# The norm tails of a two-layer hybrid block: the root taken on ScalarE straight from PSUM, token factors spread by repeated-column matmuls, residual adds dealt to GpSimd and VectorE in turn

## The reference

```python
def rmsnorm(x, g):
    y = xf * lax.rsqrt(jnp.mean(xf * xf, axis=-1, keepdims=True) + EPS)
    return y * g
def modulate(h, g_pre, shift, scale):
    return rmsnorm(h, g_pre) * (1 + scale) + shift
def gated_residual(h, y, g_post, gate, weight):
    return h + weight * gate * rmsnorm(y, g_post)
def swiglu_half(h, m, k, g_pre, g_post, wg, wu, wd):
    u = modulate(h, g_pre, m[3 * k], m[3 * k + 1])
    y = (jax.nn.silu(u @ wg) * (u @ wu)) @ wd
    return gated_residual(h, y, g_post, m[3 * k + 2], MACARON_WEIGHT)
# each layer: swiglu_half, then a mixer (state-space scan, two gated convolutions, output product)
# with its own modulate and gated_residual, then swiglu_half again; m comes from silu(c) @ w_mod + b_mod
```

## Time and profile before

| What | Value |
|---|---|
| Median of 3 runs | 2484.2 us (2481.6 to 2488.03) |
| The profiled execution: own time | 2481.05 us |
| The profiled execution: span of the rows | 2479.3 us |
| Instructions in it | 28910 |
| TensorE busy | 2263.5 us, 91% |
| VectorE busy | 1303.8 us, 53% |
| ScalarE busy | 986.9 us, 40% |
| GpSimd busy | 74.9 us, 3% |

### The profile page before, as it was taken

How to read it: one execution, slowest core, us unless ns; L and a number is a source line. 1 busy time by engine, 2 the same in 40 slices (tenths; PEclk the granted TensorE clock), 3 DMA queues, 4 the chain that set the end, 5 groups by cost and what they waited for, 6 DMA issues and landing times. The chain is left out here.

```text
span 2479.3 us, 28910 instructions
## 1 busy us (share of the span) xinstructions
PE 2263.5 (91%) x11863; PEld 1909.0 (77%) x11863; DVE 1303.8 (53%) x1785; ACT 986.9 (40%) x1479; POOL 74.9 (3%) x80
## 2 busy tenths in 40 slices
PE   5899999978998989799999997999996988978998
PEld 5788888757686767578888875888885866877997
DVE  4544444267958834544444435333325587855554
ACT  4544334244342343444433444223324442355443
POOL 0000000010101000100000001000001001000000
PEclk8999999978999989799999997999997899988999
DMA  6445544211211112244554441323321221233653
GB/s 211 145 161 170 161 158 150 93 53 51 68 35 41 49 65 85 68 153 158 165 169 155 160 144 51 102 91 96 128 94 53 69 85 52 79 109 119 188 183 124
DMA packets 275347, 278.36 MB, mean 112 GB/s; under 512 B 7487, under 2 KB 274447, under 8 KB 275215
## 3 DMA queue, kind: packets, MB, share of 16 engines
q1 hardware_dynamic: 274419, 274.32, 34.8%
q10 hardware_dynamic: 795, 2.18, 0.2%
HBM read 275.44 MB, written 1.05 MB: 112 GB/s over the span
## 5 line engine op out<-in xcount | busy, mean ns | idle before, releaser
L95 DVE TENSOR_TENSOR split<-raw,split 128x1024 fp32r<-128x1024 f32 (+1 forms) x368 | 442.7, 1203 | 744.7 <-ACT split L87 744.6
L87 ACT ACTIVATE split<-raw 128x1024 fp32r<-128x1024 f32 (+1 forms) x368 | 383.0, 1041 | 909.4 <-PE bank L128 897.4
L126 PE MATMUL bank<-uh,split 128*128 128x512 f32 (+1 forms) x1344 | 490.2, 365 | 1.2 <-DVE split L95 1.2
L128 PE MATMUL bank<-uh,split 128*128 128x512 f32 (+1 forms) x1344 | 489.3, 364 | 0.0
L127 PE MATMUL bank<-ul,split 128*128 128x512 f32 (+1 forms) x1344 | 487.5, 363 | 0.0
L128 PEld LDWEIGHTS bank<-uh,split 128*128 128x128 f32 x1344 | 252.4, 188 | 42.3
L126 PEld LDWEIGHTS bank<-uh,split 128*128 128x128 f32 x1344 | 252.5, 188 | 38.6 <-issue 1.5
L127 PEld LDWEIGHTS bank<-ul,split 128*128 128x128 f32 x1344 | 252.2, 188 | 38.8
L126 PE MATMUL bank<-mix_uh,split 128*128 128x512 f32 (+1 forms) x608 | 234.0, 385 | 32.3 <-DVE split L95 17.2
L126 PE MATMUL bank<-hh,split 128*128 128x512 f32 (+1 forms) x704 | 257.4, 366 | 1.0 <-DVE split L95 1.0
L127 PE MATMUL bank<-hl,split 128*128 128x512 f32 (+1 forms) x704 | 256.0, 364 | 0.0
(11 more groups left out here) (227 smaller groups left out, 2807.5 us busy)
## 6 DMA issues: line engine op xcount, KB each, us to landing
raw_mod<-in_w_mod SPq DMA_DIRECT2D x64, 1024.0 KB, 5.0
raw<-in_ffn_w_gate SPq DMA_DIRECT2D x44, 1024.0 KB, 5.3
raw<-in_ffn_w_up SPq DMA_DIRECT2D x44, 1024.0 KB, 5.3
raw<-in_w_in SPq DMA_DIRECT2D x40, 1024.0 KB, 5.3
raw<-in_ffn_w_down SPq DMA_DIRECT2D x32, 1024.0 KB, 5.2
raw<-in_w_out SPq DMA_DIRECT2D x16, 1024.0 KB, 5.2
raw<-in_ffn_w_down SPq DMA_DIRECT2D x16, 768.0 KB, 4.4
stage<-in_w_mod SPq DMA_DIRECT2D x6, 1024.0 KB, 12.3
```

The lines of the kernel that those rows point to most:

```text
L87: ins = K.nc.scalar.activation(K.wh[:, half, 0:kn, :], K.raw[:, slot, 0:kn, half * P:half * P + P], ACT.Copy)
L95: ins = K.nc.vector.tensor_tensor(K.wl[:, half, 0:kn, :], K.raw[:, slot, 0:kn, half * P:half * P + P], r32(K.wh[:, half, 0:kn, :]), ALU.su ...
L126: K.nc.tensor.matmul(bank[:, 0:tn], K.wh[:, half, k, :], h, start=first and k == 0, stop=False)
L128: ins = K.nc.tensor.matmul(bank[:, 0:tn], K.wl[:, half, k, :], h, start=False, stop=last and k == kn - 1)
```

## The change

There are four edits.

1. The norm factor. ScalarE now takes the root of sum/width + EPS directly from `bank[5]` (EPS as a bias tile that GpSimd fills in the opening), VectorE the reciprocal of the result into `rstd`.
2. The spread. No diagonal is built. Four matmuls (two with 256 tokens) take column t of `rstd`, repeated 128 times, as weights and the 128x128 identity as moving tile, and write 128 columns of `bank[6]` each.
3. The residual. VectorE multiplies all 8 tiles as before, but tiles 2, 5 and 7 go to `bank[0]` to `bank[2]`, and VectorE adds each from there to `K.res` right away. GpSimd adds tiles 0, 1, 3, 4 and 6.
4. The `gain` for the next phase's norm is formed in the `OutProduct` before (in the opening for the first), not at the head of the phase.

```diff
-def rstd_dve(K, dve, tok, width, stats, nth):
+def rstd_act(K, act, tok, width, stats, nth):
     n = tok[1] // P
-    dve.wait_ge(K.stat_done.sem, K.stat_done.at(stats))
-    ins = K.nc.vector.tensor_scalar(K.ms[:, 0:n], K.bank[5][:, 0:n], 1.0 / width, EPS, ALU.mult, ALU.add)
-    ins.then_inc(K.dve_step.inc(), 1)
-    dve.wait_ge(K.dve_step.sem, K.dve_step.own())
-    K.nc.vector.reciprocal(K.ms[:, 0:n], K.ms[:, 0:n]).then_inc(K.ms_ready.inc(), 1)
-    dve.wait_ge(K.rstd_ready.sem, K.rstd_ready.at(nth))
-    ins = K.nc.vector.tensor_tensor(
-        K.diag[:, 0:n, :], K.ident[:, :].unsqueeze(1).to_broadcast([P, n, P]),
-        K.rstd[:, 0:n].unsqueeze(2).to_broadcast([P, n, P]), ALU.mult)
-    ins.then_inc(K.diag_ready.inc(), 1)
-
-
-def rstd_act(K, act, tok, nth):
+    act.wait_ge(K.stat_done.sem, K.stat_done.at(stats))
+    ins = K.nc.scalar.activation(K.ms[:, 0:n], K.bank[5][:, 0:n], ACT.Sqrt, scale=1.0 / width, bias=K.eps[:, 0:1])
+    ins.then_inc(K.ms_ready.inc(), 1)
+
+
+def rstd_dve(K, dve, tok, nth):
     n = tok[1] // P
-    act.wait_ge(K.ms_ready.sem, K.ms_ready.at(nth))
-    K.nc.scalar.activation(K.rstd[:, 0:n], K.ms[:, 0:n], ACT.Sqrt).then_inc(K.rstd_ready.inc(), 1)
+    dve.wait_ge(K.ms_ready.sem, K.ms_ready.at(nth))
+    if nth > 1:
+        dve.wait_ge(K.rb_ready.sem, K.rb_ready.at(nth - 1))
+    K.nc.vector.reciprocal(K.rstd[:, 0:n], K.ms[:, 0:n]).then_inc(K.rstd_ready.inc(), 1)
 
 
 def rstd_pe(K, pe, tok, nth):
 
-    n = tok[1]
-    pe.wait_ge(K.diag_ready.sem, K.diag_ready.at(nth))
-    ins = K.nc.tensor.matmul(K.bank[6][:, 0:n], K.ones[:, :],
-                             K.diag[:, 0:n // P, :].rearrange("p t n -> p (t n)"), start=True, stop=True)
+    pe.wait_ge(K.rstd_ready.sem, K.rstd_ready.at(nth))
+    for t in range(tok[1] // P):
+        ins = K.nc.tensor.matmul(K.bank[6][:, t * P:t * P + P], K.rstd[:, t:t + 1].to_broadcast([P, P]), K.ident[:, :],
+                                 start=True, stop=True)
     ins.then_inc(K.rb_ready.inc(), 1)
...
+def pre_gain_dve(K, dve, layer, which):
+
+    nc = K.nc
+    scale = K.mod[:, layer, 8 * (3 * which + 1):8 * (3 * which + 2), :]
+    dve.wait_ge(K.mod_evac.sem, K.mod_evac.own())
+    nc.vector.tensor_scalar(K.gain[:, :, :], scale, 1.0, None, ALU.add).then_inc(K.dve_step.inc(), 1)
+    dve.wait_ge(K.dve_step.sem, K.dve_step.own())
+    g = K.par[:, layer, 0, 72 + 8 * which:80 + 8 * which].unsqueeze(2).to_broadcast([P, 8, 2])
+    nc.vector.tensor_tensor(K.gain[:, :, :], K.gain[:, :, :], g, ALU.mult).then_inc(K.dve_step.inc(), 1)
...
-POOL_TILES = 5
+POOL_TILES = (0, 1, 3, 4, 6)
+OWN_TILES = (2, 5, 7)
...
-    normed(range(6))
-    pair(0)
-    normed((6, 7))
-    add(range(POOL_TILES, 6))
-    pair(1)
-    add((6, 7))
-    pair(2)
-    pair(3)
+    own = 0
+    for j in range(8):
+        if j in POOL_TILES:
+            K.nc.vector.tensor_tensor(y[:, j, 0:tn], y[:, j, 0:tn], K.bank[6][:, 0:tn], ALU.mult).then_inc(K.yr_ready.inc(), 1)
+            continue
+        part = K.bank[own][:, 0:tn]
+        own += 1
+        K.nc.vector.tensor_tensor(part, y[:, j, 0:tn], K.bank[6][:, 0:tn], ALU.mult).then_inc(K.yb_ready.inc(), 1)
+        dve.wait_ge(K.yb_ready.sem, K.yb_ready.at(own))
+        ins = K.nc.vector.tensor_tensor(K.res[:, j, t0:t0 + tn], K.res[:, j, t0:t0 + tn], part, ALU.add)
+        ins.then_inc(K.res_tail.inc(), 1)
+        if j == 5:
+            pair(0)
+    for i in range(1, 4):
+        pair(i)
...
+            if n == 2 and self.next_norm:
+                pre_gain_dve(K, dve, *self.next_norm)
```

More of the change, by code:

```diff
@@ L329, in normed @@
         ins.then_inc(K.un_ready.inc(), 1)
[L332 to L337, removed]
     normed(0)
@@ L378, in post_tile_dve, with residual_dve @@
     K.nc.vector.tensor_tensor(total, total, more, ALU.add).then_inc(K.sq_added.inc(), 1)
-POOL_TILES = 5
-def residual_dve(K, dve, tok, y, stats, nth, norm_follows, norms_before):
+POOL_TILES = (0, 1, 3, 4, 6)
+OWN_TILES = (2, 5, 7)
+def residual_dve(K, dve, tok, y, nth, norm_follows, norms_before):
     t0, tn = tok
[L388 to L396, removed]
     def pair(i):
@@ L447, with __init__ @@
 class OutProduct:
-    def __init__(self, K, w, parts, order, xh, xl, tok, xtok, y, halves, panels, stats, norms, norm_follows, gain, mods=0,
+    def __init__(self, K, w, parts, order, xh, xl, tok, xtok, y, halves, panels, stats, norms, next_norm, gain, mods=0,
                  mod_h=0, mod_layer=0, mod_q=0):
@@ L459, in __init__ @@
         self.mods, self.mod_h, self.mod_layer, self.mod_q = mods, mod_h, mod_layer, mod_q
-        self.norm_follows, self.gain = norm_follows, gain
+        self.next_norm, self.norm_follows, self.gain = next_norm, bool(next_norm), gain
         self.mod_group = 1 if mod_h else 0
@@ L532, in act @@
                 post_tile_act(K, act, K.bank[2 * (j // 2 % 2) + j % 2], j, self.tok, self.y)
-        rstd_act(K, act, self.tok, self.norms)
+        rstd_act(K, act, self.tok, 1024, self.stats + 1, self.norms)
         if self.norm_follows:
             split_ahead_act(K, act)
-            residual_rms_act(K, act, self.tok, self.y, self.norms + 1)
+            residual_rms_act(K, act, self.tok, self.y, self.stats + 1, self.norms + 1)
     def dve(self, dve, skip=0):
@@ L557, in dve, with feed_forward @@
             mod_out_dve(K, dve, self.mod_layer, self.mod_q, self.mods // 2, self.mod_group)
-        residual_dve(K, dve, self.tok, self.y, self.stats + 1, self.norms, self.norm_follows, self.norms - 1)
+        residual_dve(K, dve, self.tok, self.y, self.norms, self.norm_follows, self.norms - 1)
         if self.norm_follows:
-            residual_rms_dve(K, dve, self.tok, self.stats + 1, self.norms + 1)
-def feed_forward(K, layer, which, tok, mod_layer, mod_q, mods_loop, mods_down, following):
+            split_ahead_dve(K, dve)
+            rstd_dve(K, dve, self.tok, self.norms + 1)
+def feed_forward(K, layer, which, tok, mod_layer, mod_q, mods_loop, mods_down, following, next_norm):
     nc = K.nc
@@ L1149, in _ @@
                         pass
-            rstd_act(K, act, part, 1)
+            rstd_act(K, act, part, GRP_T * P, GRP_T, 1)
             split_ahead_act(K, act)
@@ L1421, in _ @@
                     ins.then_inc(K.xbc_conv.inc(), 1)
-            rstd_dve(K, dve, part, GRP_T * P, GRP_T, 1)
+            rstd_dve(K, dve, part, 1)
             dve.wait_ge(K.rb_ready.sem, K.rb_ready.at(1))
@@ L1627, in _ @@
             nc.gpsimd.memset(K.cond[:, :].bitcast(F32), 0.0).then_inc(K.const_step.inc(), 1)
+            nc.gpsimd.memset(K.eps[:, :], EPS).then_inc(K.const_step.inc(), 1)
             n = K.const_step.count
@@ L1922, in hybrid_block @@
             feed_forward(K, layer, 2, LATENT if last else FULL, None if last else layer + 1, 0, not last,
-                         0 if last else 24, after)
+                         0 if last else 24, after, None if last else (layer + 1, 0))
         closing(K)
```

43 lines of the change are left out of this document (20 added, 23 removed).

## The result

The changed kernel takes **2499.4 us** (median of 5 runs, 2493.6 to 2504.2) against 2484.2 us: ratio 1.0058 (of the means, here and below), interval 1.0037 to 1.0079. It is slower by 0.6% where 0.8% less was predicted. The profiled execution took 2500.53 us, its span 2498.8.

The account below looks back on a forecast made before the run. TensorE, busy 91% of the span, bounds the kernel, so only its idle time can be won: 11.9 + 2.3 + 4.9 − 0.7 + 0.6 = 19.0 us off the 2484.2 us median gives 2465 us, range 2458 to 2477.

Parts of the forecast that it names:

- The signature: Sign that the prediction is wrong: intervals from barrier to barrier shortened while the phases between them grew; no size given.
- Norm gap: From last sum to factor spread in 16 norms: root on ScalarE without a diagonal shortens TensorE's wait, 11.9 us won.
- Spread: Factor spread on TensorE: four 128-column matmuls take less time than one of 512 columns, 2.3 us won.
- `gain`: Heads of phases: forming the pre-norm gain ahead of the barrier takes L333 and L336 off the path, 4.9 us won.
- Residual, tails with a norm: First multiply to pair 1 in four 512-token tails: the new order makes the stage 0.2 us longer each, 0.7 us lost.
- Residual, last tail: End of the kernel, where nothing follows: the new residual order shortens it from 4.75 to 4.1, 0.6 us won.
- more of the spreads fall ahead of the clock's fall: Upper bound for the four-matmul form: 5 us won if the earlier start brings two more spreads ahead of the clock's fall.
- the walk: VectorE's new residual order followed operation by operation from the first multiply: pair 1 done at 8.75 us.
- rival 1: Multiplies into PSUM ahead of pair 1 in the tails are dear: 10.8 us come in full, 2476 us; chance 0.08.
- rival 3: VectorE from first multiply to pair 1: PSUM write and add reading it both slow, about 2488 us at x = 0.75; chance 0.03.
- Rival 2, the clock: TensorE's restarts in tails and pauses meet the clock's course differently: 7 us of gain given back, 2472 us; chance 0.09.

Follow-up runs that it names:

- −64 bytes: Kernel before with only the small tensor gain allocated ahead of split, so the distance from weights to moving tensors is 64 bytes shorter: 2478.6 us, ratio 0.9977.

## Why the prediction was wrong

The step that failed is not a term of the sum. It is that the sum has none for the products: it takes 19 us off the profiled span and lets all else stand. EPS was read as "a bias tile that GpSimd fills in the opening", hence work of an instruction, and its 32 bytes were never counted. They moved every moving operand against the weights. The bodies paid 28.0 us for it (2225.2 against 2197.2 with EPS in `ms`), the dead tile alone 29 by the medians. None of the four rivals had it. The signature stood in the prediction, "the intervals from barrier to barrier shortened while the phases between them grew", but it was tied to no mechanism, and the only rival that lengthened other stretches was the clock; the granted clock is 1.00 in both bodies.

The terms, from the run with EPS in `ms` against before:

| Term | Predicted | Measured | How |
|---|---|---|---|
| Norm gap, 16 norms | 11.9 | 11.7 | last sum to spread: 8 times 1.43 to 0.57, twice 1.43 to 0.74, the rest smaller |
| Spread | 2.3 | 0.3 | all 16 spreads: 25.5 us before, 25.2 after |
| `gain` | 4.9 | 4.9 | spread to first product, five phases: 22.6 us before, 17.7 after |
| Residual, tails with a norm | −0.7 | −1.1 | first multiply to the end of the sums: four times 13.98 to 14.20, once 7.69 to 7.88 |
| Residual, last tail | +0.6 | +0.6 | 4.75 before, 4.14 in the changed kernel |
| Sum | 19.0 | 16.4 | |
| By the medians | 19.0 | 13.5 | interval 10.7 to 16.6 |

- **Norm gap.** The size was right. The root from PSUM with a bias tile takes 0.26 us, not 0.20 as in the earlier trace rows, so the gap is 0.56 or 0.57 and not 0.50; the 256-token norms gave some of that back.
- **Spread.** Mis-sized. Cold (0.50, 1.2 GHz) the eight records take 2.08 us, where I had put half of the closing's sixteen, 1.9; the 512-column matmul took 2.07. The form wins nothing. Nor did more of the spreads fall ahead of the clock's fall: in the run with EPS in `ms` two took 1.16 us, where two of before took 1.13 and 1.47.
- **`gain`.** Right: TensorE's wait from the spread to the first product fell by 1.58 and 2.08 at the two mixer starts and by 0.42 in the three other phases. With `gain` back it grew by 1.59, 1.59 and three times 0.42 or 0.43, 4.5 in all, since at the second mixer the operation then met the memsets for less time (1.34 us, not 1.80). The memsets held neither first multiply nor first low part: L339 at 520.48 took 0.69 beside the memset of 520.38.
- **Residual.** Right in kind, 0.2 us a tail; the fifth tail, which the term left out, lost as much. The difference of the edges, 128.9 against 129.6, is inside their scatter. The last tail's timeline of VectorE in the changed kernel, for the earlier trace rows; GpSimd's last add ends with it, at 2490.97:

```profile
2486.83 0.75 DVE L395 TENSOR_TENSOR y<-y,bank 128x256 f32<-128x256 f32 x2 [0.87 <-PE bank L269]
...
2490.53 0.42 DVE L401 TENSOR_TENSOR res<-res,bank 128x256 f32<-128x256 f32 x1
```

  Pair 1 came 8.92 us behind the first multiply (8.8 by the walk, 8.6 before). A write to PSUM costs what a read does: rival 1 and its 10.8 us are out, and rival 3's mechanism with it.
- **Rival 2, the clock.** True in one phase, small. In the second feed-forward of layer 0 TensorE waits longer for modulation chunks. TensorE in the kernel before, then in that with the old residual order, followed by the latter's windows (us; busy of PE, PEld, DVE, ACT, POOL; granted clock; DMA):

```profile
1068.50 1.21 PE L189 MATMUL bank<-mod_split,cond 128*128 128x256 f32 x8 [0.71 <-DVE mod_split L172]
```

```profile
1063.87 2.07 PE L189 MATMUL bank<-mod_split,cond 128*128 128x256 f32 x8 [2.02 <-DVE mod_split L172]
```

```profile
1062.00:1064.00 2.00, 0.13 (x1) 0.13 (x1) 1.23 (x1) 1.98 (x3) 0.00 (x0) 0.97 0.31 100
1064.00:1066.00 2.00, 2.00 (x9) 2.00 (x10) 1.23 (x1) 0.00 (x0) 0.00 (x0) 0.50 0.00 0
```

The wait grows from 0.71 to 2.02 us and the clock falls to 0.50 behind it; before, it stayed at 1.00. In the run with EPS in `ms` this wait is 0.91. Near the phase's end stands another such wait, here before and in the run shown:

```profile
1451.86 1.21 PE L189 MATMUL bank<-mod_split,cond 128*128 128x256 f32 x8 [1.46 <-DVE mod_split L172]
```

```profile
1450.18 2.08 PE L189 MATMUL bank<-mod_split,cond 128*128 128x256 f32 x8 [2.84 <-DVE mod_split L172]
```

It is 2.66 to 2.95 us in all five kernels that have EPS moved and the distance of before. This body is 428.0 us with EPS ahead of `split` (where the clock held), 429.2 with EPS in `ms`, 431.9 in the run shown, and 426.4 before: 1.6 to 5.5 us given back. That the shorter edge makes the chunks late is my reading; no run delayed the one without the other. What else lies between 16.4 and 13.5 is inside the interval and stays open.

Open is also which access collides. ScalarE and VectorE write `split` while TensorE reads its weights from it, and both would move with it; no run held one fixed and moved the other, nor did one move the moving operands apart from the other tensors of the phases. The Trainium skill (SBUF — State Buffer, "Who interferes with whom") gives TensorE two read ports, one for the moving operand and one for weight loads, independent of each other, and lets nothing but the port pair of VectorE and GpSimd contend. By that rule the distance between `split` and the moving operand could not matter. The measurement decides: it costs up to 8.15 us in 357.50, and up to 2.9 in 186.6 with 256 columns.

## What to carry to other kernels

An edit that adds a tile, of whatever size, moves all tensors allocated behind it, and that is a change of its own: compare the allocations of the two programs before the instructions, and put small tiles into spare columns or ahead of both buffers, as the kernel with EPS ahead of `split` did. When the trace shows the edited stretches shorter and untouched ones longer at the same granted clock, test it with a dead tile in the old kernel. Where weights are rewritten beside long streams of products, try a few distances between the two buffers: here the best and the worst of eight lie 1.35% of the whole time apart. Measure the whole kernel, since products of another width can like another distance.

## What the runs showed of the hardware

- The pace of fp32r products at full clock depends on the distance in SBUF between the weights' buffer and the tensors of the phases, the moving operands among them. Over shifts by 32 to 256 bytes the body with 1536 products of 512 columns took 354.2 to 365.7 us, 7.4 ns each between the ends, and that with 1536 products of 256 columns 184.5 to 189.5 us, 3.3 ns each. The two orders differ: −64 bytes is the best for 512 columns and the worst for 256.
- VectorE writes to PSUM at the pace of SBUF, 0.69 us for 128x512, and an add that reads the tile just written takes 0.69 too.
- A [128, 4] root on ScalarE takes 0.26 us from PSUM with a bias tile, 0.20 from SBUF without.
- Four 128-column matmuls with a repeated column as weights take as long as one with 512 columns: 2.08 against 2.07 us at clock 0.50, 1.16 against 1.13 at 1.00.
